# A two-layer transformer kernel: the memory's keys and values are computed inside the loop over the score maps

## The reference

```
u = rms_norm(h, norm_mix)
qa, ka, va, qb, kvb, gb, gate_a, gate_b = split(u @ w_in)
o_a = diff_attention(qa, ka, va)                # 4 heads x 2 score maps
o_b = nsa_attention(qb, kvb, sigmoid(gb))       # compressed, selected, window: 8 heads x 2 maps
merged = sigmoid(gate_a) * (o_a @ w_branch_a) + sigmoid(gate_b) * (o_b @ w_branch_b)
h = h + merged @ w_out
m = rms_norm(mem, norm_mem)                     # 256 x 1024, needs nothing of h
k, v = split(m @ w_cross_kv)
h = h + softmax((rms_norm(h, norm_cross) @ w_cross_q) @ k.T / sqrt(128)) @ v @ w_cross_o
h = h + peer_ffn(rms_norm(h, norm_ffn))         # keys, top 16, 128 rows of uv per token gathered
return rms_norm(h, norm_final)
```

## Time and profile before

| | |
|---|---|
| median of 3 runs (lowest, highest) | 1564.78 us (1564.63, 1565.46) |
| the profiled execution's own time | 1564.94 us |
| its span | 1562.8 us |
| PE, PEld, DVE, ACT, POOL busy | 81%, 48%, 48%, 30%, 17% |
| granted TensorE clock, mean | 0.913 of full speed |
| HBM traffic | 542.66 MB, 347 GB/s over the span |

### The profile page before, as it was taken

How to read it: one execution, slowest core, us unless ns; L and a number is a source line. 1 busy time by engine, 2 the same in 40 slices (tenths; PEclk the granted TensorE clock), 3 DMA queues, 4 the chain that set the end, 5 groups by cost and what they waited for, 6 DMA issues and landing times.

```text
span 1562.8 us, 21200 instructions
## 1 busy us (share of the span) xinstructions
PE 1268.1 (81%) x8509; PEld 744.5 (48%) x8509; DVE 742.9 (48%) x1768; ACT 468.2 (30%) x1248; POOL 273.3 (17%) x287
## 2 busy tenths in 40 slices
PE   7999999999999887988999887678755645655556
PEld 7787656665555447976666544245411111111112
DVE  5544212221121116357641666575767676767454
ACT  5832111110010016455542134242323232323222
POOL 1000000000000001000000133334443333333341
PEclk9999999999999998989999989989977687687778
DMA  9448999999999995542162399999999999999996
GB/s 368 161 182 355 427 423 427 426 422 428 424 425 425 424 401 225 201 177 108 66 258 93 149 397 422 421 390 399 421 421 421 420 421 421 421 421 421 422 421 270
DMA packets 64438, 544.09 MB, mean 348 GB/s; under 512 B 6608, under 2 KB 7120, under 8 KB 12368
## 3 DMA queue, kind: packets, MB, share of 16 engines
q1 hardware_dynamic: 26016, 273.84, 42.6%
q0 software_dynamic: 38016, 268.45, 41.7%
q10 hardware_dynamic: 304, 0.39, 0.1%
HBM read 541.61 MB, written 1.05 MB: 347 GB/s over the span
## 4 chain that ended last, share of the span: by engine, by line
PE 42%; DMA 40%; DVE 8%; ACT 5%; issue 4%; POOL 1%; DVEq 0%; POOLq 0%; SPq 0%; ACTq 0%
PE PS L197 41%; DMA AR<-in_uv,CO 25%; DMA AR<-in_w_up 12%; DVE AR L2267 2%; DMA Wk<-in_w_up 2%; PE PS L207 2%; ACT HI L186 1%; DVE Wk L1593 0%; POOL AR L2476 0%; DMA XN<-in_uv,CO 0%; ACT Wk L2169 0%; ACT SM L2163 0%; DVE Wk L1596 0%; DVE LO L193 0%; DMA CO<-in_const 0%
## 5 line engine op out<-in xcount | busy, mean ns | idle before, releaser
L197 PE MATMUL PS<-AR,Wk 64*64 64x512 f32 (+4 forms) x2288 | 430.0, 726 | 198.5 <-ACT Wk L2169 185.9
L2267 DVE CUSTOM_DVE_ANT_0 AR<-AR,PS 128x1024 f32<-128x1024 f32 x210 | 255.6, 1220 | 186.5 <-DMA AR<-in_uv,CO 168.5
L197 PEld LDWEIGHTS PS<-AR,Wk 64*64 64x64 f32 (+3 forms) x2288 | 120.1, 159 | 456.3 <-ACT Wk L2169 293.4
L2476 POOL DMA_INDIRECT AR<-in_uv,CO x202 | 193.6, 958 | 318.4 <-PE PS L197 279.6
L197 PE MATMUL PS<-AR 128*64 128x256 f32 (+3 forms) x1944 | 220.3, 383 | 16.9 <-DMA AR<-in_w_up 13.9
L197 PEld LDWEIGHTS PS<-AR 128*64 128x64 f32 (+2 forms) x1944 | 137.0, 139 | 105.5 <-DMA AR<-in_w_up 20.3
L308 POOL TENSOR_TENSOR ST<-ST 128x2 f32<-128x2 f32 (+3 forms) x14 | 11.3, 807 | 802.5 <-DVE ST L1114 477.5
L2159 ACT ACTIVATE RW<-SM 128x2 f32<-128x2 f32 (+1 forms) x132 | 27.0, 205 | 394.3 <-DVE SM L2267 375.5
L197 PE MATMUL PS<-Wk,AR 128*128 128x128 f32 (+2 forms) x976 | 114.7, 308 | 4.3 <-DMA Wk<-in_w_up 2.2
L197 PEld LDWEIGHTS PS<-Wk,AR 128*128 128x128 f32 (+1 forms) x976 | 98.8, 176 | 34.7 <-issue 17.3
L992 DVE TENSOR_TENSOR AR<-AR,PS 128x256 f32<-128x256 f32 x32 | 13.5, 422 | 199.5 <-ACT AR L849 199.5
(11 more groups left out here) (295 smaller groups left out, 1651.3 us busy)
## 6 DMA issues: line engine op xcount, KB each, us to landing
AR<-in_w_gate SPq DMA_DIRECT2D x28, 2048.0 KB, 14.8
AR<-in_w_up SPq DMA_DIRECT2D x27, 2048.0 KB, 14.7
AR<-in_w_down SPq DMA_DIRECT2D x27, 2048.0 KB, 14.7
AR<-in_w_in SPq DMA_DIRECT2D x14, 2048.0 KB, 10.1
Wk<-in_w_up SPq DMA_DIRECT2D x5, 2048.0 KB, 14.7
Wk<-in_w_down SPq DMA_DIRECT2D x5, 2048.0 KB, 14.7
Wk<-in_w_gate SPq DMA_DIRECT2D x4, 2048.0 KB, 14.7
AR<-in_w_pq SPq DMA_DIRECT2D x4, 2048.0 KB, 8.5
```

The lines of the kernel that those rows point to most:

```text
L197: return pe.matmul(o, l, r, start=start, stop=stop, skip_group_check=True)
L2267: t = dve.tensor_tensor_reduce(r, r, P(6 if g < 128 else 2, 2), 1.0, 0.0, ALU.mult, ALU.add, DT[:, g:g + 1])
L2476: pool.indirect_dma_start(RING[k], None, uv, bass.IndirectOffsetOnAxis(ap=IDX[:, g:g + 1], axis=0)).then_inc(g_in[k], 16)
```

## The change

1. **Gates from step 0.** `spare` is gone. g00 and g01 lie in steps 0 to 5 (9, 9 and 6 matmuls), the other six gates take two steps each (12 and 12), steps 6 to 17 (`unit_part`, `unit_pe`).
2. **The memory in the loop.** Its square sums are taken in step 12, it is scaled in steps 13 and 14, turned in steps 16 and 17 (`tm0`, `tm1`, banks 4 and 5) and split by ACT and DVE (`y`); its keys are steps 18 to 21 (`mk`), its values steps 22 to 25 (`mv`). The square sums and `oturn` of the first attention come a step earlier.
3. **Weights.** ACT makes the high parts of b6's first two quarters before it evacuates `vb`; b7, b8 and b9 are split from steps 2, 6 and 10, kv0 in 15 and 16, kv1 in 19 to 21. kv1 is loaded into slot 3 once g31 is done, cq and co once mk3 is, o20 and pq0 once mv1 is.
4. **Behind the loop.** No memory work is left there. PE makes a00, a01, b00, b01, a10, `tx0`, a11, r00, r10, `tz0`, cq0, sc0, b10, b11, `pt0`, `pv0`, w00, w10, `tp0`. The sigmoids of the first half of the gates lie in step 23. GT lies elsewhere in SBUF.

```diff
-                ("wb", rows4(w_b), 1, None), ("kv0", w_ckv[0], 2, 0), ("o20", w_out2[0], 3, None), ("o21", w_out2[1], 7, None),
-                ("kv1", w_ckv[1], 8, 1), ("cq", w_cq[0], 2, None), ("co", rows4(w_co), 4, None), ("pq0", w_pq[0], 5, None),
+                ("wb", rows4(w_b), 1, None), ("kv0", w_ckv[0], 2, 0), ("kv1", w_ckv[1], 3, 1), ("o21", w_out2[1], 7, None),
+                ("cq", w_cq[0], 2, None), ("co", rows4(w_co), 4, None), ("o20", w_out2[0], 3, None), ("pq0", w_pq[0], 5, None),
...
         b_act_names = [*split_steps("b0"), "xs1", *eights("x"), *split_steps("b1"), *fours("q"), "lam", *split_steps("b2"),
                        *fours("k"), *split_steps("b3"), *twos("va"), *split_steps("b4"), *fours("qb"), *split_steps("b5"), *fours("kv"),
-                       *twos("vb"), "gt"]
+                       "b6.0", "b6.1", *twos("vb"), "gt"]
...
-        FIRST_GATE = 3
-        gate_highs = {1: ("b6", (0, 1)), 2: ("b6", (2, 3)), **{5 + k: ("b7", (k,)) for k in range(4)},
-                      **{10 + k: ("b8", (k,)) for k in range(4)}, **{16 + k: ("b9", (k,)) for k in range(4)}}
-
-        def gate_part(n):
-
-            k, part = (n - FIRST_GATE) // 3, (n - FIRST_GATE) % 3
-            return k, ((0, 3), (3, 6), (6, 8))[part]
+        HIGHS = {0: ("b6", (2, 3)), **{2 + q: ("b7", (q,)) for q in range(4)}, **{6 + q: ("b8", (q,)) for q in range(4)},
+                 **{10 + q: ("b9", (q,)) for q in range(4)}, 15: ("kv0", (0, 1)), 16: ("kv0", (2, 3)), 19: ("kv1", (0,)), 20: ("kv1", (1,)),
+                 21: ("kv1", (2, 3))}
+        HIGHS_BEHIND = {"b8": "g01", "b9": "g11", "kv0": "g21", "kv1": "g31"}
+
+        def low_step(n):
+
+            return n if n < 2 else n - 1
+
+        def unit_part(n):
+
+            if n < 6:
+                return "g", n // 3, ((0, 3), (3, 6), (6, 8))[n % 3]
+            if n < 18:
+                return "g", n // 2 - 1, ((0, 4), (4, 8))[n % 2]
+            if n < 22:
+                return "k", n - 18, (0, 8)
+            if n < 26:
+                return "v", n // 2 - 11, ((0, 4), (4, 8))[n % 2]
+            return None, None, (0, 0)
+
+        def unit_done(n):
+
+            kind, k, (_, c1) = unit_part(n) if n >= 0 else (None, None, (0, 0))
+            return ({"g": f"g{k // 2}{k % 2}", "k": f"mk{k}", "v": f"mv{k}"}[kind], kind, k) if c1 == 8 else (None, None, None)
...
-                               ("kv0", b_pe.at("g21")), ("o20", b_pe.at("g31")),
-                               ("o21", b_pe.at("g31")), ("kv1", b_pe.at("val23"))):
+                               ("kv0", b_pe.at("g21")), ("kv1", b_pe.at("g31")), ("o21", b_pe.at("g31")),
+                               ("cq", b_pe.at("mk3")), ("co", b_pe.at("mk3")), ("o20", b_pe.at("mv1")), ("pq0", b_pe.at("mv1"))):
                 sp.wait_ge(*step)
                 load_piece(sp, name)
...
+            def unit_pe(n):
+                kind, k, (c0, c1) = unit_part(n)
+                xs = slice(k % 2 * 128, k % 2 * 128 + 128) if kind else None
+                if kind == "g":
+                    j, tt = k // 2, k % 2
+                    wh, wl = halves_of(f"b{6 + j}")
+                    if c0 == 0 and k:
+                        pe.wait_ge(*b_act.at(f"g{(k - 1) // 2}{(k - 1) % 2}"))
+                    for c in range(c0, c1):
+                        if tt == 0 and c % 2 == 0:
+                            pe.wait_ge(*b_dve.at(f"b{6 + j}.{c // 2}"))
+                        t = three(pe, P(3), X2[0][:, c, xs], X2[1][:, c, xs], wh[:, c, :], wl[:, c, :], c == 0, c == 7)
+                elif kind == "k":
+                    if k >= 2:
+                        pe.wait_ge(*b_act.at(f"mk{k - 2}"))
+                    if k == 0:
+                        pe.wait_ge(*b_dve.at("y7"))
+                    t = turned(pe, "kv0", MX2, P(4 + k % 2)[:, 0:256], k, *((b_dve,) if k == 0 else ()))
+                elif kind == "v":
+                    wh, wl = halves_of("kv1")
+                    if c0 == 0:
+                        pe.wait_ge(*b_act.at(f"mk{2 + k}"))
+                    for c in range(c0, c1):
+                        if k == 0 and c % 2 == 0:
+                            pe.wait_ge(*b_dve.at(f"kv1.{c // 2}"))
+                        t = three(pe, P(4 + k), MX2[0][:, c, xs], MX2[1][:, c, xs], wh[:, c, :], wl[:, c, :], c == 0, c == 7)
+                if unit_done(n)[0]:
+                    t.then_inc(*b_pe.up(unit_done(n)[0]))
+
             for n in range(27):
                 if n < 24 and n % 2 == 0:
                     if n:
...
+                unit_pe(n)
...
+                elif n == 16:
+                    pe.wait_ge(*b_dve.at("oat"))
+                    pe.wait_ge(*b_act.at("mem1"))
+                    memory_turned_pe(0).then_inc(*b_pe.up("tm0"))
+                elif n == 17:
+                    pe.wait_ge(*b_dve.at("y3"))
+                    memory_turned_pe(4).then_inc(*b_pe.up("tm1"))
...
             high_quarters(act, "b5", b_act)
             evac(kV, "kv", (2, 3, 2, 3))
+            high_quarters(act, "b6", b_act, range(2))
             for tt in range(2):
                 act.wait_ge(*b_pe.at(f"vb{tt}"))
                 act.activation(VB[:, tt, :], P(6 + tt)[:, 0:280], ACT.Copy).then_inc(*b_act.up(f"vb{tt}"))
...
+                        act.activation(MX2[0][:, c, :], memory_chunk(c), ACT.Copy, scale=sm["g_mem"][:, c:c + 1]).then_inc(*b_act.up(f"y{c}"))
+                elif n == 23:
+                    act.wait_ge(*b_act.at("g31"))
+                    sigmoids(act, 0)
+                if n in HIGHS:
+                    name, quarters = HIGHS[n]
+                    if name in HIGHS_BEHIND:
+                        act.wait_ge(*b_pe.at(HIGHS_BEHIND[name]))
+                    high_quarters(act, name, b_act, quarters)
...
+            sp.wait_ge(*b_pe.at("val23"))
+            sp.dma_start(SKS, subk.rearrange("p (a n) -> p a n", a=16)).then_inc(ld_sk, 16)
+            sp.dma_start(GROW, gp).then_inc(ld_gp, 16)
+            sp.wait_ge(*l_pe.at("b11"))
+            load_piece(sp, "pq1")
 
         def halves_pe(pe):
-            pe.wait_ge(*b_dve.at("mem"))
-            pe.wait_ge(*b_act.at("g31"))
-            turn_pe(pe, MM, l_pe, "turnm")
+            pe.wait_ge(*b_dve.at("oat"))
+            pe.wait_ge(*b_act.at("mv1"))
+            pe.wait_ge(*arrived("wa"))
+            for j in range(2):
+                branch_pe(pe, "a", 0, j, 4 + j).then_inc(*l_pe.up(f"a0{j}"))
             pe.wait_ge(*b_act.at("ob"))
-            pe.wait_ge(*b_dve.at("oat"))
-            pe.wait_ge(*arrived("wa"))
             pe.wait_ge(*arrived("wb"))
             for j in range(2):
...
+                branch_pe(pe, "b", 0, j, 6 + j).then_inc(*l_pe.up(f"b0{j}"))
+            branch_pe(pe, "a", 1, 0, 0).then_inc(*l_pe.up("a10"))
+            pe.wait_ge(*l_dve.at("sx01"))
+            turn_half_pe(pe, SGA[:, 0, :], (2, 3), l_pe.up("tx0"))
+            branch_pe(pe, "a", 1, 1, 1).then_inc(*l_pe.up("a11"))
             pe.wait_ge(*l_act.at("x0"))
             pe.wait_ge(*l_dve.at("x0"))
             pe.wait_ge(*arrived("o20"))
             out_pe(pe, "o20", 0, 4).then_inc(*l_pe.up("r00"))
...
             out_pe(pe, "o21", 0, 5).then_inc(*l_pe.up("r10"))
-            branch_pe(pe, "a", 1, 0, 6).then_inc(*l_pe.up("a10"))
             pe.wait_ge(*l_dve.at("h01"))
             turn_half_pe(pe, H[:, 0, :], (2, 3), l_pe.up("tz0"))
-            branch_pe(pe, "b", 1, 0, 7).then_inc(*l_pe.up("b10"))
             pe.wait_ge(*l_act.at("z0"))
             pe.wait_ge(*l_dve.at("z0"))
...
             pe.wait_ge(*arrived("cq"))
-            heads_pe(pe, "cq", 0, 0, range(4)).then_inc(*l_pe.up("cq0"))
-            tokens(pe, "kv1", MX2, P(4), 0, l_dve).then_inc(*l_pe.up("v0"))
+            heads_pe(pe, "cq", 0, 4, range(4)).then_inc(*l_pe.up("cq0"))
             pe.wait_ge(*l_act.at("cqt0"))
             scores_pe(pe, (2, 3)).then_inc(*l_pe.up("sc0"))
-            tokens(pe, "kv1", MX2, P(5), 1).then_inc(*l_pe.up("v1"))
+            for j in range(2):
+                branch_pe(pe, "b", 1, j, 6 + j).then_inc(*l_pe.up(f"b1{j}"))
             pe.wait_ge(*l_dve.at("soft0"))
-            maps_turned_pe(pe, 0, (0, 1)).then_inc(*l_pe.up("pt0"))
+            maps_turned_pe(pe, 0, (4, 5)).then_inc(*l_pe.up("pt0"))
             pe.wait_ge(*l_act.at("cpt0"))
             memory_pe(pe, 0, 2).then_inc(*l_pe.up("pv0"))
...
-            cross_out_pe(pe, 1, 0).then_inc(*l_pe.up("w10"))
-            branch_pe(pe, "a", 1, 1, 4).then_inc(*l_pe.up("a11"))
-            branch_pe(pe, "b", 1, 1, 5).then_inc(*l_pe.up("b11"))
+            cross_out_pe(pe, 1, 4).then_inc(*l_pe.up("w10"))
             pe.wait_ge(*l_dve.at("w10"))
-            turn_half_pe(pe, H[:, 0, :], (1, 2), l_pe.up("tp0"))
+            turn_half_pe(pe, H[:, 0, :], (5, 2), l_pe.up("tp0"))
             pe.wait_ge(*l_act.at("p0"))
             pe.wait_ge(*l_dve.at("p0"))
```

204 lines of the change are left out of this document (82 added, 122 removed).

## The result

Eleven executions of the changed kernel against eleven of the kernel before: median 1570.91 us (1566.74 to 1574.69) against 1564.65 (1561.32 to 1569.72), ratio 1.004 with a 95% interval of 1.0027 to 1.0053. So the change makes the kernel slower by 6.3 us (4.2 to 8.3).

A forecast was written before the change was run, and what follows sets the result against it. The gathers were taken as the bound to the end, so the change is worth what it moves `tp0`, behind a stretch of almost only PE. +5.0 + 19.8 - 21.0 = +3.8 us on 1564.94 gave 1568.7 us, range 1562.0 to 1574.0.

The forecast's parts named there:

- The first steps: Loop's start to step 3's gate: 5.0 us later, as vb's evacuation and the gates wait for b6; bounds from 4.0.
- The rest of the loop: Behind step 3: 19.8 us longer, from 19.1 of PE work, 1.6 of waits and -0.9 for the clock.
- The waits: PE's waits in the loop behind step 3, mostly at gate boundaries: 11.1 us in place of 9.5, +1.6.
- Behind the loop: Loop's end to `tp0`: 21.0 us shorter, 24.6 of memory work gone less 3.6 of uncovered waits.
- The four waits: PE's waits between the loop's end and `tp0` that lose their cover: 3.6 us in sum, bounds 2.8 and 5.0.
- One to one to the end: From `tp0` through the gathers to the end: whatever moves `tp0`'s start moves the end by as much.
- The clock: Steps 3 to 5: the lower level (0.66 in 690 to 695 us) was expected to stay.
- The first burst at half clock: Rival, chance 0.16: gate matmuls and `cmp` in steps 0 and 1 at half rate, 2.8 us more, 1571.5 us.
- the forecast's own case: Whole kernel: 3.8 us slower, 1568.7 us, own range 1565.3 to 1573.5, chance 0.42; clock low in steps 3 to 5.
- Full clock in steps 3 to 5: Rival, chance 0.14: gate matmuls of steps 0 to 5 keep the clock up, 4.8 us less, 1563.9 us.
- The sum: Whole kernel: +5.0 + 19.8 - 21.0 = +3.8 us, 1568.7 us; bounds +0.4 to +8.6.

The follow-up runs named there:

- The first experiment: Changed kernel with ACT evacuating vb and making GT ahead of b6's first two high parts: 1570.34 us against 1564.37, ratio 1.0037.
- gate copies first: Changed kernel with the high parts of odd steps 3 to 15 and step 11's square sums put off behind the next step's exps: 1566.59 us, ratio 1.0013.
- branches spread: Changed kernel with a10 and a11 cut in parts and laid over PE's waits behind the loop: 1568.49 us against 1563.02, ratio 1.0035.
- three repairs: Changed kernel with cmp ahead of the gates, a10 and a11 spread over waits, gates copied ahead of pt: 1554.84 us against 1564.05, ratio 0.9934.

## Why the prediction was right, step by step, and where it was not

**The first steps (+5.0).** Measured + 6.4 in the profiled execution and + 5.3 to 5.5 in three variants that left this stretch alone or filled it. First scores + 3.7 (3.8 said), the wait ahead of `key` 3.50 (3.5 said); in between, the second half of `cmp` ended 5.8 us later behind vb, where 4.7 were said. The number held, its reason did not whole: "PE waits for it before the first scores, so the loop starts ... 3.8 us later" named ACT's order as the cause. The first experiment took that away and gained nothing, since DVE's `tk` and PE's own gate matmuls stood behind b6 as well. I had read the one wait that ends last and not what would be last next. So the forecast of this term was right in size and half right in mechanism.

**The rest of the loop (+19.8).** Measured + 19.2. The waits: 11.1 said, 11.1 measured; 2.3 at the square sums and at kv0 were 2.19 and 2.10, the boundaries with one high part 0.85 to 1.19, the one for `y` 1.8 in place of 1.2. That the whole stretch agrees within 0.6 is partly luck: the changed kernel's loop took 114.4 to 116.1 us in four profiles that left it alone, and the kernel before's 92.3, 96.5 and 97.2 in three, so the difference is anything from 17 to 24 us by the pair that is taken.

**Behind the loop (-21.0).** Measured - 20.0: this term was mis-sized. The four waits came as idle times of 0.79, 1.27, 0.69 and 0.78, 3.5 in sum for the 3.6 that I took. The missing us lies in the work: leaving out the bracketed waits, PE's stretch shrank from 88.29 - 1.86 = 86.4 to 68.29 - 5.40 = 62.9 us, by 23.5 in place of 24.6. The pieces next to the new waits grew. `tz0`, for one, took 843.21 to 844.37 us, where the wait behind it begins: 1.16 us, in place of 0.89 in the kernel before:

```profile
824.76 1.05 PE L207 MATMUL PS<-CO,Hs 128*128 128x128 f32 x8
825.65 3.60 PE L197 MATMUL PS<-AR,Wk 128*128 128x512 f32 x8
```

There the next piece starts 0.16 us ahead of its modelled end. Read in the same way, r00 and r10 grew by 0.15, cq0 by 0.31, sc0 by 0.29, w00 and w10 by 0.16: with `tz0` 1.2 us, enough for the whole of it. Filling three waits of 2.75 us gave 3.17, so a part of this comes back with the waits.

**One to one to the end.** Shown by the table, to within 3 us.

**The clock.** "The first burst at half clock" did happen in the profiled execution, so there the forecast's own case was wrong and that rival right. Its 1571.5 us even comes nearer to the result than 1568.7, but by luck: its price of 2.8 us was too high, 1.1 in this profile, and 0.4 up to `key` where only the gate matmuls fell under it. The rule of the Trainium skill (page "TensorE: Matmul & The Clock Gate", section "HAM oscillation — how this bites in real kernels") says that after an idle gap the next burst starts at half rate; the trace agrees: behind 4.17 us of idle time the granted clock was 0.50 from 670 to 675 us, and with spare matmuls in that place 1.00. It agrees less sharply elsewhere: behind 3.95 and 4.02 us of idle time (gate copies first, branches spread) the first scores still took 0.93 us, and the clock fell behind them, to 0.66 over the same 5 us. The prediction's remark that waits shorter than 2.32 were followed by no fall was a misreading: 1.15 us stood ahead of 0.66, as it says itself. What the burst costs is set by who waits for it. "Full clock in steps 3 to 5" did not come, as forecast.

**The sum.** + 3.8 said; the terms measured give 6.4 + 19.2 - 20.0 + 0.1 = + 5.7, and the medians + 6.3 (4.2 to 8.3). The miss of 1.9 is 1.4 in the first steps, 1.0 behind the loop, less 0.6 in the loop. The remaining 0.6 is less than the medians can tell. The sum is small beside its terms of 20, so its sign hung on each of them being right to a few us.

## What to carry to other kernels

When a load's consumers are moved ahead, list every queue that then stands behind its landing, on each engine, and not only the wait that the trace shows last: taking one away moves the wait to the next. A change that moves much work for little time may still be worth keeping, if the order around it is put right: here + 6.3 us became - 9.2 by three repairs that moved nothing between the loop and its tail. Cut independent work to the size of the waits that it is to fill, and let a copy that frees a bank stand in a step where nothing on its engine waits for others.

## What the hardware showed that I had not expected

The same program met the lower clock at different places from one execution to the next: in the kernel before with b6's parts moved, the loop behind step 3 took 92.27 us in one and 97.16 in another. The waits of 1.18, 0.69, 0.78 and 1.27 us around `tp0` left the clock at 1.00 in five profiles of versions of the changed kernel; in three others the queries behind them took 7.22 us in place of 5.60. Executions of one kernel spread over 3 to 9 us, which is as much as the change moves; stretches of a trace, taken from a common mark, told terms of 1 us apart that medians of ten executions could not, except where the clock itself had moved. Why those three fell, all of them versions with moved gate copies, stays open.
